# One core's decoder step: memory values projected onto rows, dt on column quarters, one memory chunk in another group

## The chip, the cores and the metric

The kernel runs as one program on one core of a Trainium2 chip. The metric is the device time of one execution in microseconds (us). TensorE (PE) does the matrix products, VectorE (DVE) and ScalarE (ACT) the elementwise work, GpSimd (POOL) only issues transfers here, and SyncE (SP) issues the loads of the weights.

## The reference

A two-layer decoder step over 320 tokens (256 of a prompt, 64 of eight samples), all in float32. Cut to what the change touches:

```python
h = rmsnorm(x)
z, xbc, dt_raw, q, k, v, g = split(h @ w_in)
dt = softplus(dt_raw + dt_bias)              # 16 heads
xbc = silu(causal_conv(xbc, ...))            # 12 slices of 128 channels
... SSD scan (uses the running sum of dt * A), retention, new states ...
x = x + concat(y_ssd, y_ret) @ w_out
mem_k = mem @ w_mk;  mem_v = mem @ w_mv      # 256 memory rows, 1024 columns each; both are outputs
x = x + cross_attend(rmsnorm(x), mem_k, mem_v)
x = x + hier_moe(rmsnorm(x))
```

## The kernel before

Activations lie with features on the 128 partitions and the 320 tokens along the free axis. All weights come as one stream of pieces of 2 MB ("quads"), numbered `q` in the order in which SP loads them into a ring of three slots (some more slots later in the layer). SP works through the list strictly in order: before a load it waits until the slot that the quad goes to is free (`freed[s]`). PE waits for `loaded[s]` in `quad(...)`, and frees a slot with the first matmul that follows its last use (`free`, `first`). A product of `h` with 128 weight columns is 8 matmuls of 128x320 in `products` (L563).

**dt.** After the 12 products for xBC, 8 matmuls with 16 weight columns each (L618) give dt_raw, then `project(Q_Z, ...)` goes on with z. ACT copies dt_raw out of PSUM, DVE does softplus and the running sum on 16 partitions (L1653 to L1678), and then the 12 convolutions (L1687, L1691).

**The memory chunks.** mem_k and mem_v are 16 products of 8 matmuls of 128x256 each, called chunks 0 to 15 here. PE does them in `project_memory(n)`, strewn as filler between the small steps of the states; ACT copies each out (L1306). Chunks 0 to 3 use quad 12, 4 to 7 quad 14, 8 to 11 quad 17, 12 to 15 quad 19. Between these, quads 13, 15, 16 and 18 hold the samples' incoming states. In the ring of three, quad 17 takes the slot of quad 14, quad 18 that of 15, and quad 19 that of 16, so quad 17 can be loaded only when chunk 7 is done.

**The four groups of sample states** (k = 0 to 3, the loop ahead of L881). In each, PE runs `from_states(k)` (L825), `new_states(k, 0)` (L857 or L860), a memory chunk, `turn_off(k)` (8 transposes, L837), `new_states(k, 1)`, with one more chunk behind k = 0 and one inside k = 3. `new_states` with running number u waits for `s_newst`, DVE's `state_half` of number u - 1 (L1874, or L1880 and L1887), since it writes the same PSUM banks. When DVE is through with a state quad, it frees its slot.

**mem_v.** Chunks 8 to 15 give mem_v with features on partitions; attention needs it with memory rows on partitions. So `turn_values` turns it with 4 times 4 transposes on PE (L902) between the products of `w_out` (L917), and ACT copies the turned parts to `v_mem`.

Of the kernel before, what the change touches and what calls it, by code (L numbers as in the profile page):

```python
# [19 lines left out]
ACT = mybir.ActivationFunctionType  # L20
# [3 lines left out]
P = 128  # L24
# [134 lines left out]
def build(nc, stream, params, consts, x_in, mem_in, y_out, st_out, conv_out, mk_out, mv_out):  # L159
    with ExitStack() as ctx:  # L160
# [3 lines left out]
        def sem(name):  # L164
            return ctx.enter_context(nc.semaphore(name))
# [70 lines left out]
        wide = view(work, 5376, 3, GB * P)  # L236
        vt_mem = view(work, 16196, KD, M)

        v_mem = view(work, 0, 2, D)
        q_all = view(work, 2048, KD, T)  # L240
# [120 lines left out]
        s_mkvout = sem("s_mkvout")  # L361
        s_vt = sem("s_vt")
        s_vtout = sem("s_vtout")
        s_mkstore = sem("s_mkstore")
# [161 lines left out]
        def _(pe):  # L526
# [56 lines left out]
            def mixer(L):  # L583
# [309 lines left out]
                project_memory(16 - n_mem)  # L893
                pe.wait_ge(s_mkvout, (L + 1) * 16)

                def turn_values(i):

                    mc, half = i // 2, i % 2
                    if i >= 2:
                        pe.wait_ge(s_vtout, L * 4 + i - 1)  # L900
                    for c in range(4):
                        mm = pe.transpose(psum[:, 4 + half, c * P:(c + 1) * P],  # L902
                                          vt_mem[:, 4 * half + c, mc * P:(mc + 1) * P], ident)
                        if c == 0:
                            first(mm)
                    mm.then_inc(s_vt, 1)

                for j in range(KD):
                    w = quad(pe, L, Q_OUT + j // 2)
                    if j >= 4:  # L910
                        pe.wait_ge(s_xadd, L * 16 + j - 3)
                    for i in range(2 * KD):
                        if j == 0 and i % KD == 0:
                            pe.wait_ge(s_mix, L * 2 + i // KD + 1)
                        a = (j % 2) * 2 * SLAB + i * P
                        src = xbc[:, i, :] if i < KD else kq[:, i - KD, :]
                        mm = pe.matmul(psum[:, j % 4, 0:T], w[:, a:a + P], src, start=(i == 0), stop=(i == 15))  # L917
                        if i == 0:
                            first(mm)
                    mm.then_inc(s_wout, 1)  # L920
                    if j % 2 == 1:
                        free(Q_OUT + j // 2)
                    if 2 <= j < 6:
                        turn_values(j - 2)

            def attention(L):

                pe.wait_ge(s_vtout, (L + 1) * 4)

# [339 lines left out]
        def _(act):  # L1269
# [22 lines left out]
            def mixer(L):  # L1292
# [7 lines left out]
                def memory(chunks):  # L1300
                    nonlocal n_mem
                    for _ in range(chunks):
                        c = n_mem
                        act.wait_ge(s_mkv, L * 16 + c + 1)
                        dst = k_mem[:, c, :] if c < KD else vt_mem[:, c - KD, :]
                        act.activation(dst, memory_out(c), ACT.Copy).then_inc(s_mkvout, 1)  # L1306
                        n_mem += 1
                nt = 0
# [14 lines left out]
                for c in range(CC):  # L1323
# [6 lines left out]
                    n_evac += 1  # L1330
                evac(dt_tmp[0:H, 0, :], rows_=H)

# [129 lines left out]
                for j in range(KD):  # L1462
                    if 2 <= j < 6:
                        i = j - 2
                        act.wait_ge(s_vt, L * 4 + i + 1)
                        act.activation(v_mem[:, i // 2, (i % 2) * BANK:(i % 2 + 1) * BANK], psum[:, 4 + i % 2, :],
                                       ACT.Copy).then_inc(s_vtout, 1)
                    act.wait_ge(s_xadd, L * 16 + j + 1)
                    square(L, 1, j)
# [105 lines left out]
        def _(dve):  # L1575
# [31 lines left out]
            def mixer(L):  # L1607
# [72 lines left out]

                for c in range(CC):
                    dve.wait_ge(s_evac, L * 29 + c + 1)
                    if c >= 2:
                        dve.wait_ge(s_silu, L * CC + c - 1)
                    a = conv_acc[:, c % 2, :]
                    wa, ba = PAT["conv_w"] + c * CW, PAT["conv_b"] + c
                    dve.tensor_scalar(a, raw[:, c, 0:XOUT], par[:, L, wa:wa + 1], par[:, L, ba:ba + 1],  # L1687
                                      ALU.mult, ALU.add)
                    for j in range(1, CW):
                        dve.drain()  # L1690
                        ins = dve.scalar_tensor_tensor(out=a, in0=raw[:, c, j:j + XOUT],  # L1691
                                                       scalar=par[:, L, wa + j:wa + j + 1], in1=a,
                                                       op0=ALU.mult, op1=ALU.add)
                    ins.then_inc(s_conv, 1)
                dve.tensor_copy(conv_tail[:, :, 0:CW - 1], raw[:, :, XS0 - (CW - 1):XS0])
# [470 lines left out]
        def _(pool):  # L2166
            for L in range(DEPTH):
# [24 lines left out]
                pool.wait_ge(s_mkvout, L * 16 + 8)  # L2192
                pool.dma_start(mk_out[L], k_mem[:]).then_inc(s_mkstore, 16)
                pool.wait_ge(s_mkvout, L * 16 + 16)
                pool.dma_start(mv_out[L], vt_mem[:]).then_inc(s_mvstore, 16)
            for i in range(3):
# [115 lines left out]
```

## Time and profile before

| | |
|---|---|
| median of 3 runs | 1607.63 us (1606.44 to 1610.14) |
| the profiled execution, whole | 1604.76 us |
| its span, first to last instruction | 1603.0 us |
| PE busy | 1535.9 us, 96% of the span |
| DVE, ACT busy | 539.6 us, 292.4 us |
| mean granted TensorE clock | 0.989 |
| loaded and stored in all | 387.77 MB, mean 242 GB/s |

The profiled execution lies 2.87 us under the median of the runs. Busy time of PE counts an instruction from its start to its modelled end. The two layers are alike; layer 0 has its state groups at 280 to 323 us, layer 1 at 1069 to 1112 us. In counts of PE rows, a matmul and its weight load are two instructions: x16 is 8 matmuls.

### The profile page before, as it was taken

The page shows a single profiled execution, that of the slowest core. Times are in us where ns is not written, and L with a number is a line of the kernel's source. Part 1 is how long each engine was busy: PE and PEld are TensorE (multiplying, and loading weights), DVE is VectorE, ACT ScalarE, POOL GpSimd, SP SyncE. Part 2 cuts the span into 40 slices and gives each one's busy share as a digit, 9 for nine tenths or more (in the row PEclk, how much of TensorE's full clock was granted, in tenths as well). Part 3 has the DMA queues.
Part 4 walks back from the last instruction along what each step waited for, and adds up shares of the span by engine and source line. Part 5 has one row for each costly group of instructions (what it writes and reads, how often), then busy time and mean ns, then how long its engine had stood idle before and what let it go on. Part 6 is the DMA issues. An engine that isn't in the chain of part 4 may idle for free.

```text
span 1603.0 us, 20261 instructions
## 1 busy us (share of the span) xinstructions
PE 1535.9 (96%) x8652; PEld 979.8 (61%) x8652; DVE 539.6 (34%) x1110; ACT 292.4 (18%) x614; POOL 28.0 (2%) x56
## 2 busy tenths in 40 slices
PE   7999999899999999999999998998999999999997
PEld 5776668577766554445367776685776675444543
DVE  3304654561132411211323065636412423121122
ACT  2013322140121301001100142212311212000102
POOL 0000000000000000000000000000000000000000
PEclk9999999999999999999999999998999999999999
DMA  7233322884267599999723242329733757999991
GB/s 312 105 117 146 136 93 101 320 326 173 105 244 302 234 414 404 404 402 410 283 80 131 105 159 97 132 106 358 298 139 135 303 212 315 403 404 409 408 395 60
DMA packets 31262, 387.77 MB, mean 242 GB/s; under 512 B 3776, under 2 KB 4224, under 8 KB 6592
## 3 DMA queue, kind: packets, MB, share of 16 engines
q1 hardware_dynamic: 26048, 357.74, 56.8%
q0 software_dynamic: 5120, 28.69, 4.5%
q8 instruction: 70, 1.15, 0.3%
q14 instruction: 24, 0.20, 0.0%
HBM read 361.66 MB, written 24.75 MB: 241 GB/s over the span
## 4 chain that ended last, share of the span: by engine, by line
PE 92%; DVE 3%; DMA 2%; ACT 1%; DVEq 1%; issue 1%; ACTq 0%; SPq 0%
PE psum L563 38%; PE psum L1139 14%; PE psum L917 9%; PE psum L1159 7%; PE psum L1184 5%; PE psum L1114 4%; DMA ring<-stream 2%; PE psum L579 1%; PE psum L570 1%; PE psum L1125 1%; PE psum L951 1%; PE psum L996 1%; PE psum L1014 1%; PE psum L967 1%; PE psum L764 1%; PE psum L576 1%
## 5 line engine op out<-in xcount | busy, mean ns | idle before, releaser
L563 PE MATMUL psum<-h,ring 128*128 128x320 f32 x1664 | 458.9, 436 | 0.9 <-issue 0.9
L563 PEld LDWEIGHTS psum<-h,ring 128*128 128x128 f32 x1664 | 315.8, 191 | 135.7 <-issue 9.2
L1139 PE MATMUL psum<-ring,work 128*64 128x512 f32 x768 | 170.3, 592 | 1.4 <-ACT work L1529 1.4
L563 PE MATMUL psum<-mem,ring 128*128 128x256 f32 x512 | 120.6, 391 | 7.2 <-DMA ring<-stream 7.2
L1139 PEld LDWEIGHTS psum<-ring,work 128*64 128x64 f32 x768 | 55.0, 137 | 110.2 <-issue 108.5
L563 PEld LDWEIGHTS psum<-mem,ring 128*128 128x128 f32 x512 | 97.8, 195 | 28.2 <-DMA ring<-stream 8.3
L1159 PE MATMUL psum<-work 128*64 128x512 f32 x512 | 113.4, 595 | 0.7 <-ACT work L1540 0.7
L917 PE MATMUL psum<-work,ring 128*128 128x320 f32 x384 | 104.9, 433 | 0.9 <-ACT work L1306 0.9
L917 PEld LDWEIGHTS psum<-work,ring 128*128 128x128 f32 x384 | 72.3, 190 | 30.9 <-ACT work L1306 1.8
L563 PE MATMUL psum<-work,ring 128*128 128x320 f32 x256 | 71.9, 443 | 11.7 <-DMA ring<-stream 10.5
L2062 DVE TENSOR_TENSOR x<-x,psum 128x320 f32<-128x320 f32 x128 | 62.5, 488 | 54.9 <-PE psum L1184 49.2
L1159 PEld LDWEIGHTS psum<-work 128*64 128x64 f32 x512 | 35.3, 137 | 67.5 <-issue 66.3
L1594 DVE TENSOR_TENSOR x<-x,psum 128x320 f32<-128x320 f32 x32 | 15.6, 488 | 175.7 <-PE psum L917 123.6
L1184 PE MATMUL psum<-work 128*128 128x320 f32 x256 | 73.2, 439 | 0.5 <-issue 0.5
L563 PEld LDWEIGHTS psum<-work,ring 128*128 128x128 f32 x256 | 49.8, 195 | 33.0 <-issue 13.7
L2107 DVE TENSOR_TENSOR work<-work,psum 128x512 f32<-128x512 f32 x16 | 11.0, 688 | 173.4 <-ACT work L1538 173.4
L1114 PEld LDWEIGHTS psum<-work 128*128 128x128 f32 x512 | 60.0, 196 | 13.7 <-issue 13.7
L1184 PEld LDWEIGHTS psum<-work 128*128 128x128 f32 x256 | 47.2, 190 | 31.5 <-issue 13.6
L1114 PE MATMUL psum<-work 128*128 128x128 f32 x512 | 63.0, 283 | 2.2 <-DVE work L2053 2.2
L1538 ACT ACTIVATE work<-psum 128x512 f32<-128x512 f32 x16 | 9.6, 597 | 285.6 <-PE psum L1139 285.6
L1139 PE MATMUL psum<-states_out,work 128*64 128x512 f32 x256 | 58.4, 598 | 0.0
L1326 ACT ACTIVATE work<-psum 128x256 f32<-128x256 f32 x24 | 9.2, 385 | 216.8 <-PE psum L563 216.8
(296 smaller groups left out, 1387.6 us busy)
## 6 DMA issues: line engine op xcount, KB each, us to landing
ring<-stream SPq DMA_DIRECT2D x111, 2048.0 KB, 11.0
work<-stream SPq DMA_DIRECT2D x32, 2048.0 KB, 9.9
states_out<-stream SPq DMA_DIRECT2D x24, 2048.0 KB, 9.6
st_out<-states_out POOLq DMA_DIRECT2D x12, 1024.0 KB, 11.4
st_out<-work POOLq DMA_DIRECT2D x6, 1024.0 KB, 7.5
work<-acum_flat POOLq DMA_DIRECT2D x10, 256.0 KB, 3.9
k_mem<-acum_flat POOLq DMA_DIRECT2D x10, 256.0 KB, 3.5
ring<-stream SPq DMA_DIRECT2D x4, 512.0 KB, 9.2
```

The source lines that it names most:

```text
L563: mm = pe.matmul(out, w[:, a:a + P], rhs[:, j, :], start=(j == 0), stop=(j == KD - 1))
L570: mm = pe.transpose(o, i, ident[0:i.shape[0], 0:i.shape[0]])
L576: return pe.transpose(out, src[:, cols(t)], ident)
L579: mm = pe.matmul(out[32 * j:32 * j + DS, :], src[:, own:own + DS], ident, start=True, stop=True, skip_group_check=True)
L764: mm = pe.matmul(o, x_of[t][:, hd * HD:(hd + 1) * HD], dec[:, 0, hh * n:(hh + 1) * n], start=True, stop=(t != 1), skip_group_check=True)
L917: mm = pe.matmul(psum[:, j % 4, 0:T], w[:, a:a + P], src, start=(i == 0), stop=(i == 15))
L951: mm = pe.matmul(psum[:, t, rr * M:(rr + 1) * M], q_all[:, k, tok(t)], k_mem[:, k, :], start=(c == 0), stop=(c == 1))
L1114: mm = pe.matmul(psum[:, 4 + half, i * P:(i + 1) * P], h_tok[:, t, j * P:(j + 1) * P], chosen[:, p, t, :], start=(i + t == 0), stop=False, ...
L1139: mm = pe.matmul(psum[ab * CAP:(ab + 1) * CAP, up, :], h_packed[:, p % 2, k, ab * CAP:(ab + 1) * CAP], w[:, a:a + BANK], start=(k == 0), s ...
L1159: mm = pe.matmul(psum[ab * CAP:(ab + 1) * CAP, 2 + half, :], hidden_t[:, f, ab * CAP:(ab + 1) * CAP], w[:, a:a + BANK], start=(f == 0), st ...
L1184: pe.matmul(psum[:, SPREAD[j % 4], 0:T], y_pair[:, j * P:(j + 1) * P], picked_t, start=True, stop=True).then_inc(s_spread, 1)
L2062: dve.tensor_tensor(x[:, j, :], x[:, j, :], psum[:, SPREAD[j % 4], 0:T], ALU.add)\
```

## The change

It has three parts, the same in both layers.

1. **Values on rows.** The weights of mem_v are laid out in another order, and chunks 8 to 15 become eight half sums of 4 matmuls of 128x512: 128 memory rows are the stationary side, 512 columns of `w_mv` stream. Two chunks together give one block of `v_mem` in its final layout, and ACT copies only after each second chunk. `v_mem` takes the place in SBUF that the unturned values had. The 16 transposes of `turn_values`, their waits and their copies are gone. The same number of columns streams as before.
2. **dt on quarters.** The 8 matmuls of dt write four quarters of the PSUM partitions, two sums in each. ACT copies all 128 rows, PE does the first z product meanwhile, then adds up the quarters in one more matmul with a constant (`fold`), and ACT copies its 16 rows. DVE does convolutions 0 and 1 ahead of the dt chain instead of behind it.
3. **One chunk moves.** The extra chunk behind group k = 0 now stands behind group k = 2. The chunks keep their order, so group 0 has chunk 5, group 1 chunk 6, and group 2 chunks 7 and 8 (before: 5 and 6, 7, and 8).

```diff
 def memory_out(c):
     if c < 2:
         return psum[:, 0, 0:M]
-    return psum[:, 7, 0:M] if c >= 6 and c % 2 == 0 else psum[:, 4, M:2 * M]
+    if c >= KD:
+        return psum[:, (7, 4)[(c - KD) // 2 % 2], :]
+    return psum[:, 7, 0:M] if c == 6 else psum[:, 4, M:2 * M]
...
 # TensorE, dt
-    mm = pe.matmul(psum[0:H, n_proj % 4, 0:T], w[:, j * H:(j + 1) * H], h[:, j, :],
-                   start=(j == 0), stop=(j == KD - 1))
+    q = 32 * (j % 4)
+    mm = pe.matmul(psum[q:q + H, n_proj % 4, 0:T], w[:, j * H:(j + 1) * H], h[:, j, :],
+                   start=(j < 4), stop=(j >= 4), skip_group_check=True)
...
-project(Q_Z, range(2))
+project(Q_Z, [0])
+pe.wait_ge(s_tables, 16)
+pe.wait_ge(s_evac, L * 29 + 13)
+pe.matmul(psum[0:H, 4, 0:T], k_("fold", H), dt_tmp[:, 5, :], start=True, stop=True).then_inc(s_dtfold, 1)
+project(Q_Z, [1])
+pe.wait_ge(s_dtrow, L + 1)
...
 # TensorE, project_memory
-elif c > 6:
-    pe.wait_ge(s_mkvout, L * 16 + c - 1)
-products(memory_out(c), w, (c % 4) * SLAB, P, mem).then_inc(s_mkv, 1)
+elif 6 < c < KD:
+    pe.wait_ge(s_mkvout, L * 12 + c - 1)
+elif c >= KD and c % 2 == 0:
+    pe.wait_ge(s_mkvout, L * 12 + 7 + (c - KD) // 2)
+if c < KD:
+    products(memory_out(c), w, (c % 4) * SLAB, P, mem).then_inc(s_mkv, 1)
+else:
+    mt = (c - KD) // 2 % 2
+    for k in range(4 * (c % 2), 4 * (c % 2) + 4):
+        mm = pe.matmul(memory_out(c), mem[:, k, mt * P:(mt + 1) * P],
+                       w[:, k * BANK:(k + 1) * BANK], start=(k == 0), stop=(k == KD - 1),
+                       skip_group_check=True)
+        if k % 4 == 0:
+            first(mm)
+    if c % 2 == 1:
+        mm.then_inc(s_mkv, 1)
...
 # TensorE, the groups of states
     new_states(k, 1)
-    if k == 0:
+    if k == 2:
         project_memory(1)
...
 # TensorE, between the products of w_out
-        if 2 <= j < 6:
-            turn_values(j - 2)
...
 # ScalarE
-evac(dt_tmp[0:H, 0, :], rows_=H)
+evac(dt_tmp[:, 5, :])
+act.wait_ge(s_dtfold, L + 1)
+act.activation(dt_tmp[0:H, 0, :], psum[0:H, 4, 0:T], ACT.Copy).then_inc(s_dtrow, 1)
...
-memory(3)
+memory(2)
 act.activation(gate[:], gate[:], ACT.Silu)
 off_to_tok(2)
-memory(2)
+memory(3)
...
 # VectorE
+convolve(0)
+convolve(1)
 dve.wait_ge(s_proj, L * 45 + 29)
...
-dve.wait_ge(s_evac, L * 29 + 13)
+dve.wait_ge(s_dtrow, L + 1)
```

PE's rows in the groups of states, from `new_states(0, 1)` to `new_states(2, 1)`, before. Here `mem,ring 128x256 x8` is a chunk, L825 is `from_states`, L837 is `turn_off`, and L857 and L860 are `new_states`.

```order
L857 MATMUL psum<-states_out 128x256 x8
L563 MATMUL psum<-mem,ring 128x256 x8
L825 MATMUL psum<-ring,work 8x512 x8
L860 MATMUL psum<-h 128x512 x4
L563 MATMUL psum<-mem,ring 128x256 x8
L837 MATMUL psum<-cst,h 128x128 x8
L860 MATMUL psum<-h 128x512 x4
L825 MATMUL psum<-ring,h 8x256 x16
L857 MATMUL psum<-work 128x256 x8
L563 MATMUL psum<-mem,ring 128x256 x8
L837 MATMUL psum<-cst,h 128x128 x8
L857 MATMUL psum<-work 128x256 x8
```

The same stretch in the changed kernel, where L568 and L714 are chunks, L850 is `from_states`, L862 `turn_off`, and L882 and L885 `new_states`.

```order
L882 MATMUL psum<-states_out 128x256 x8
L850 MATMUL psum<-ring,work 8x512 x8
L885 MATMUL psum<-h 128x512 x4
L568 MATMUL psum<-mem,ring 128x256 x8
L862 MATMUL psum<-cst,h 128x128 x8
L885 MATMUL psum<-h 128x512 x4
L850 MATMUL psum<-ring,h 8x256 x16
L882 MATMUL psum<-work 128x256 x8
L568 MATMUL psum<-mem,ring 128x256 x8
L862 MATMUL psum<-cst,h 128x128 x8
L882 MATMUL psum<-work 128x256 x8
L714 MATMUL psum<-ring,mem 128x512 x4
```

Between `new_states(0, 1)` and `from_states(1)` the chunk is gone; chunk 7, the last user of quad 14, now stands behind `new_states(2, 0)`, and chunk 8, the first of quad 17, behind `new_states(2, 1)`.

PE's rows around dt before, from xBC's products to the first transposes of the values of retention (L576, L579); L618 is dt.

```order
L563 MATMUL psum<-h,ring 128x320 x160
L618 MATMUL psum<-h,ring 16x320 x8
L563 MATMUL psum<-h,ring 128x320 x16
L576 MATMUL psum<-cst,work 128x128 x16
L579 MATMUL psum<-cst,work 8x128 x64
```

And in the changed kernel, where L624 is dt and L634 the matmul with `fold`.

```order
L568 MATMUL psum<-h,ring 128x320 x160
L624 MATMUL psum<-h,ring 16x320 x8
L568 MATMUL psum<-h,ring 128x320 x8
L634 MATMUL psum<-work,cst 16x320
L568 MATMUL psum<-h,ring 128x320 x8
L581 MATMUL psum<-cst,work 128x128 x16
```

One z product now stands between dt and the matmul that completes it, and one behind.

## Rows read from the trace of the kernel before

**Rows 1.** The page: busy time by engine, and the chain that ended last.

```profile
PE 1535.9 (96%) x8652; PEld 979.8 (61%) x8652; DVE 539.6 (34%) x1110; ACT 292.4 (18%) x614; POOL 28.0 (2%) x56
...
PE 92%; DVE 3%; DMA 2%; ACT 1%; DVEq 1%; issue 1%; ACTq 0%; SPq 0%
```

**Rows 2.** Stages: busy time by engine; last three: granted clock, DMA share, GB/s.

```profile
283.00:323.00 40.00, 32.42 (x238) 21.14 (x231) 24.66 (x22) 6.70 (x8) 3.21 (x6) 0.91 0.80 306
308.00:310.00 2.00, 0.00 (x0) 0.00 (x0) 1.43 (x2) 0.00 (x0) 0.24 (x1) 0.64 0.97 406
546.00:800.00 254.00, 250.04 (x1337) 120.18 (x1338) 59.02 (x121) 28.56 (x49) 0.00 (x0) 1.00 0.94 381
```

**Rows 3.** The chain that ended last, in time: start, length, what; both layers.

```profile
299.44 11.73 DMA ring<-stream
...
1089.77 11.23 DMA ring<-stream
```

**Rows 4.** PE's timeline, groups of states, layer 0; in brackets the wait ahead.

```profile
302.19 1.91 PE L825 MATMUL psum<-ring,h 128*8 128x256 f32 x32 [0.45 <-DMA ring<-stream]
305.77 1.15 PE L857 MATMUL psum<-work 8*128 8x256 f32 x16 [1.67 <-DVEq L1888]
311.22 5.76 PE L563 MATMUL psum<-mem,ring 128*128 128x256 f32 x16 [4.30 <-DMA ring<-stream]
...
321.50 1.14 PE L860 MATMUL psum<-work 8*128 8x512 f32 x8 [0.74 <-DVEq L1888]
```

**Rows 5.** The chain, in time: widths 512 and 256, and products of w_out.

```profile
246.26 1.73 PE psum L704 x4
...
343.94 10.37 PE psum L563 x48
...
381.31 8.61 PE psum L917 x32
390.37 8.62 PE psum L917 x32
```

**Rows 6.** PE's timeline, the same stretch, layer 1.

```profile
1096.09 2.09 PE L857 MATMUL psum<-work 8*128 8x256 f32 x16 [0.67 <-DVEq L1888]
1101.04 5.10 PE L563 MATMUL psum<-mem,ring 128*128 128x256 f32 x16 [2.86 <-DMA ring<-stream]
...
1110.66 1.14 PE L860 MATMUL psum<-work 8*128 8x512 f32 x8 [0.30 <-DVEq L1888]
```

**Rows 7.** Timelines: dt on PE, routing's column quarters on PE, DVE at dt.

```profile
134.04 4.48 PE L618 MATMUL psum<-h,ring 128*16 128x320 f32 x16
...
533.97 1.27 PE L1073 MATMUL psum<-work,par 128*20 128x320 f32 x14
...
139.01 0.37 DVE L1653 TENSOR_SCALAR work<-work,par 16x320 f32<-16x320 f32 x1 [29.28 <-ACT work L1313]
```

**Rows 8.** DVE's timeline, groups of states, layer 0.

```profile
289.23 2.35 DVE L1874 SCALAR_TENSOR_TENSOR states_out<-ring,psum 128x1024 f32<-128x1024 f32 x2 [0.69 <-PE psum L857]
291.80 2.29 DVE L1925 TENSOR_TENSOR work<-work 128x2048 f32<-128x2048 f32 x1 [0.21 <-issue]
...
303.40 2.29 DVE L1887 TENSOR_TENSOR work<-work,psum 128x2048 f32<-128x2048 f32 x1
```

**Rows 9.** Transfers issued 243-244, 299-301, 305-308, 347.3-348: KB, us to landing.

```profile
ring<-stream SPq DMA_DIRECT2D x1, 2048.0 KB, 7.7
...
ring<-stream SPq DMA_DIRECT2D x1, 2048.0 KB, 11.7
...
ring<-stream SPq DMA_DIRECT2D x1, 2048.0 KB, 12.7
...
states_out<-stream SPq DMA_DIRECT2D x1, 2048.0 KB, 8.2
ring<-stream SPq DMA_DIRECT2D x1, 2048.0 KB, 13.9
```

More of the change, by code:

```diff
@@ L236, in build @@
         wide = view(work, 5376, 3, GB * P)
-        vt_mem = view(work, 16196, KD, M)
-        v_mem = view(work, 0, 2, D)
+        v_mem = view(work, 16196, 2, D)
         q_all = view(work, 2048, KD, T)
@@ L312, in build @@
         s_rotated = sem("s_rotated")
+        s_dtfold = sem("s_dtfold")
+        s_dtrow = sem("s_dtrow")
         s_dtv = sem("s_dtv")
@@ L361, in build @@
         s_mkvout = sem("s_mkvout")
-        s_vt = sem("s_vt")
-        s_vtout = sem("s_vtout")
         s_mkstore = sem("s_mkstore")
@@ L463, in memory_out, with memory_taken @@
                 return psum[:, 0, 0:M]
-            return psum[:, 7, 0:M] if c >= 6 and c % 2 == 0 else psum[:, 4, M:2 * M]
+            if c >= KD:
+                return psum[:, (7, 4)[(c - KD) // 2 % 2], :]
+            return psum[:, 7, 0:M] if c == 6 else psum[:, 4, M:2 * M]
+        def memory_taken(c):
+            return c if c <= KD else KD + (c - KD) // 2
         def place_of(step):
@@ L893, in mixer @@
                 project_memory(16 - n_mem)
[L894 to L906, printed above, removed]
+                pe.wait_ge(s_mkvout, (L + 1) * 12)
                 for j in range(KD):
@@ L1303, in memory @@
                         c = n_mem
-                        act.wait_ge(s_mkv, L * 16 + c + 1)
-                        dst = k_mem[:, c, :] if c < KD else vt_mem[:, c - KD, :]
+                        n_mem += 1
+                        if c >= KD and c % 2 == 0:
+                            continue
+                        act.wait_ge(s_mkv, L * 12 + memory_taken(c + 1))
+                        u = (c - KD) // 2
+                        dst = k_mem[:, c, :] if c < KD else v_mem[:, u % 2, (u // 2) * BANK:(u // 2 + 1) * BANK]
                         act.activation(dst, memory_out(c), ACT.Copy).then_inc(s_mkvout, 1)
-                        n_mem += 1
                 nt = 0
@@ L1462, in mixer @@
                 for j in range(KD):
[L1463 to L1467, printed above, removed]
                     act.wait_ge(s_xadd, L * 16 + j + 1)
@@ L1647, in mixer, with convolve @@
                                     w[:, a:a + DB * (CW - 1)].rearrange("p (b j) -> p b j", b=DB))
+                def convolve(c):
+                    dve.wait_ge(s_evac, L * 29 + c + 1)
+                    if c >= 2:
+                        dve.wait_ge(s_silu, L * CC + c - 1)
+                    a = conv_acc[:, c % 2, :]
+                    wa, ba = PAT["conv_w"] + c * CW, PAT["conv_b"] + c
+                    dve.tensor_scalar(a, raw[:, c, 0:XOUT], par[:, L, wa:wa + 1], par[:, L, ba:ba + 1],
+                                      ALU.mult, ALU.add)
+                    for j in range(1, CW):
+                        dve.drain()
+                        ins = dve.scalar_tensor_tensor(out=a, in0=raw[:, c, j:j + XOUT],
+                                                       scalar=par[:, L, wa + j:wa + j + 1], in1=a,
+                                                       op0=ALU.mult, op1=ALU.add)
+                    ins.then_inc(s_conv, 1)
+                dve.drain()
+                convolve(0)
+                convolve(1)
                 dve.wait_ge(s_proj, L * 45 + 29)
@@ L1679, in mixer @@
                     .then_inc(s_dtv, 1)
[L1681 to L1694, printed above, removed]
+                for c in range(2, CC):
+                    convolve(c)
                 dve.tensor_copy(conv_tail[:, :, 0:CW - 1], raw[:, :, XS0 - (CW - 1):XS0])
@@ L2191, in _ @@
                     pool.dma_start(st_out[L, 1 + u], new_of[STORE_SLOT[u]]).then_inc(s_store[STORE_SLOT[u]], 16)
-                pool.wait_ge(s_mkvout, L * 16 + 8)
+                pool.wait_ge(s_mkvout, L * 12 + 8)
                 pool.dma_start(mk_out[L], k_mem[:]).then_inc(s_mkstore, 16)
-                pool.wait_ge(s_mkvout, L * 16 + 16)
-                pool.dma_start(mv_out[L], vt_mem[:]).then_inc(s_mvstore, 16)
+                pool.wait_ge(s_mkvout, (L + 1) * 12)
+                pool.dma_start(mv_out[L], v_mem[:]).then_inc(s_mvstore, 16)
             for i in range(3):
@@ L2245 @@
                  state_ret[l].transpose(2, 0, 1, 3).reshape(P, GB, 4, 1024)]
-        st[Q_MEM] = quads(slabs(np.concatenate([f(w_mk)[l], f(w_mv)[l]], 1)))
+        st[Q_MEM[:2]] = quads(slabs(f(w_mk)[l]))
+        st[Q_MEM[2:]] = f(w_mv)[l].reshape(KD, P, 2, BANK).transpose(2, 1, 0, 3).reshape(2, P, QUAD)
         for k, (ret, gb) in enumerate(STATES):
@@ L2286 @@
     outs = {"y_out": (P, KD, T), "st_out": (DEPTH, 1 + DB, P, 2048), "conv_out": (DEPTH, P, CC, (CW - 1) * (1 + DB)),
-            "mk_out": (DEPTH, P, KD, M), "mv_out": (DEPTH, P, KD, M)}
+            "mk_out": (DEPTH, P, KD, M), "mv_out": (DEPTH, P, 2, D)}
     nc = bacc.Bacc("TRN2", target_bir_lowering=False, num_devices=1)
@@ L2310 @@
     return (c(y[:SEQ].reshape(1, SEQ, D)), c(y[SEQ:].reshape(DB, DS, D)), c(ssm[:, :1]), c(conv[:, :1]), c(ret[:, :1]),
-            c(memory(r["mk_out"])), c(memory(r["mv_out"])), c(ssm[:, 1:]), c(conv[:, 1:]), c(ret[:, 1:]))
+            c(memory(r["mk_out"])),
+            c(np.asarray(r["mv_out"]).transpose(0, 2, 1, 3).reshape(DEPTH, 1, M, XH, DV)), c(ssm[:, 1:]), c(conv[:, 1:]), c(ret[:, 1:]))
```

3 lines of the change are left out of this document (1 added, 2 removed).

## Prediction

> **What bounds the kernel now.** I read the page first. PE is busy for 96% of the span, and 92% of the chain that ended last lies on it [rows 1]: whatever PE is spared in a busy stage comes off the time, and whatever it waits longer is added. In the experts' stage it is busy for 250 of 254 us [rows 2], so nothing done earlier is given back or made up there; it just begins earlier or later.
>
> The table by stage then shows the one place that is different. In the groups of states, 283 to 323 us, PE is busy for 32.4 of 40 us and transfers move 306 GB/s [rows 2]. The chain there runs through a load of the ring: 11.73 us from 299.44 in layer 0, and 11.23 us from 1089.77 in layer 1 [rows 3]. That load is quad 17, issued when chunk 7 was done. PE's timeline shows what it costs: `new_states(2, 0)` begins at 305.77, held by DVE, and then PE stands still for 4.30 us until chunk 8 can begin at 311.22 [rows 4]. Chunk 8 takes 5.76 us, where three chunks in a row take 10.37, so 3.46 each [rows 4, 5]: the granted clock, 0.64 in the mean of 308 to 310 [rows 2], has fallen to the lower level, 1.2 GHz, after PE had stood idle, and rises again during the chunk. The reader should see that the whole change hangs on this load, since the moved chunk is tied to it.
>
> As the mark by which I compare I take the end of `new_states(3, 0)`: 321.50 + 1.14 = 322.6 in layer 0 and 1110.66 + 1.14 = 1111.8 in layer 1 [rows 4, 6]. Before and after the change the same chunks remain behind it.
>
> **dt on quarters.** The 8 matmuls of 16 columns take 4.48 us [rows 7], as much as full ones. In the routing of the experts 7 matmuls of 20 columns already go to four quarters, and take 1.27 us [rows 7]; 8 would take 1.45. The added `fold` matmul has the same 320 columns as one of the old ones: 4.48 / 8 = 0.56. PE saves 4.48 - 1.45 - 0.56 = 2.5 us a layer, 5.0 in all. The new waits cost nothing while a z product hides them: it is 8 matmuls of 320 columns, so about 4.4 us, and ACT's copy of dt behind it is one instruction; without that cover it would be a copy's time twice a layer. DVE gets dt about 1.45 + 4.4 + 0.56 - 4.48 = 1.9 us later on the layer's clock. It had been idle for 29.28 us before dt [rows 7], and convolutions 0 and 1 now fall into that gap, so what follows dt starts no later.
>
> The Trainium skill ("TensorEngine Tiling (Array Packing)", Key Properties) says that a change of tiling mode drains the engine, which speaks against quarters between full products. Routing's 7 matmuls stand between full products too, and their 1.27 us leave room for 0.29 of overhead at most if they stream at a quarter of 0.56 each. By the page without a price I could not sum; by the row the saving stays.
>
> **Values on rows.** 32 matmuls of 512 columns replace 64 of 256. Two of 512 took 1.73 us [rows 5], so four take 3.46: exactly a chunk of eight. No gain, no loss on PE. What is gone is the turning: between two products of `w_out` there is a gap of 390.37 - 381.31 - 8.61 = 0.45 us [rows 5], four times a layer, so 1.75 us a layer and 3.5 in all. ACT loses its copies, which nothing waited for in time; its last copy ahead of `w_out` gets twice as wide, some tenths of a us that I count at nothing. Bounds of these two parts together: 7.0 (if `fold` and its waits cost twice) to 9.5; I take 8.5.
>
> **The moved chunk.** Group 0 has one chunk less, group 2 one more. Three things follow in order.
>
> First, nothing moves earlier for DVE. From 289.23 its state work runs almost without a break until 303.40 + 2.29 = 305.7 [rows 8], so `new_states(2, 0)` still begins at 305.8, and PE, a chunk short in groups 0 and 1, waits more for it. Second, chunk 7 now runs behind it: 305.77 + 1.15 + 3.46 = 310.4. Only then is the slot of quad 14 free, so quad 17 is issued at 310.4 instead of 299.44, eleven us later. SP takes its list in order, so quad 18, the states of group 3, is held behind it and is issued at 310.4 as well. Third, PE does `turn_off(2)` and `new_states(2, 1)` and stands at chunk 8 from about 312.4.
>
> How long do the two loads take? Alone a load landed after 7.7 us; quads 17 and 18 took 11.7 and 12.7 with stores of new states beside them; of two issued together the first landed after 8.2 and the second after 13.9, 5.7 apart [rows 9]. Here too two stores of new states go out beside them, behind `new_states(2, 0)` and `new_states(2, 1)`. I take 10.0 for quad 17, between alone and 11.7, nearer to the latter, and 15.0 for quad 18, the pair's 13.9 with a little for the stores. So quad 17 is there at 320.4, PE has been idle for 8 us, and chunk 8 at the low clock takes 5.5 (5.76 and 5.10 before [rows 4, 6]): 325.9. Quad 18 is there at 325.4. Then `from_states(3)` at 1.9 (as in [rows 4]) and `new_states(3, 0)` at 1.14, for which DVE is long ready: 328.9, or 6.3 us later than before.
>
> In layer 1 `new_states(2, 0)` begins at 1096.09. It took 2.09 there and the chunk 5.10 at the low clock [rows 6], against 1.15 and 3.46 at the high one; chunk 7 ends between 1100.7 and 1103.3, I take 1102.0. Plus 10.0, 5.1, 1.9 and 1.14: 1120.1, or 8.3 later. Together +14.6.
>
> The Trainium skill ("DMA: Bandwidth & Descriptors", Anatomy of one DMA) fits a transfer's time as 2.0 us plus its bytes at 436 GB/s. That is 6.8 us for 2 MB and 11.6 for two, both shorter than the rows' 7.7 and 13.9, and the moved chunk would then cost some 6 us less than I say. The measured rows are for this kernel's own loads, so I stay with them.
>
> Behind the mark I find no slack that takes this back: the next loads are issued by the same steps and only shift.
>
> **Sum.** +14.6 - 5.0 - 3.5 = +6.1 us on the profiled execution's 1604.76, so 1610.9. That execution lies 2.87 under the median of 1607.63; on the median's scale the sum is 1613.7 us. A measurement of this kernel can tell about 0.2%, 3.2 us, from no change.
>
> **The rivals.** What decides is the time P from the issue of quad 17 to the landing of quad 18, and the clock. At the high clock the marks come at 310.4 + P + 3.04 and 1100.7 + P + 3.04, so both layers lose 2P - 17.2 together.
>
> *The loads are quick and the clock holds.* With 7.7 and 5.7 behind it, P is 13.4; the loss of 9.6 and the gain of 8.5 cancel: 1608.7. For it speaks that the transfer queues stand nearly idle before 310 in the changed order; against it that two stores go out then, and that PE's clock fell in both layers after much less idleness. It holds up to P = 14.5.
>
> *The chunk fills the stall.* This one is faster. Chunk 7 covers the 4.30 us, and quad 17 is there when PE wants it, at 312.4. The mark would be 312.4 + 3.46 + 3.04 = 318.9, 3.7 earlier, and in layer 1 1109.2, 2.6 earlier: -6.3 - 8.5 = -14.8, so 1592.8. For it speaks that the wait is exactly where the chunk goes. Against it: the load would have to land 2 us after its slot is free. Any gain over 0.2% needs P under 11.3, and no pair in the rows was that quick.
>
> *All goes badly.* Low clock already in chunk 7 of both layers, loads of 12.7 and 5.7 behind: 334.4 and 1124.7, a loss of 24.7, net +16.2, so 1623.8.
>
> *The change doesn't do what it says for dt.* If quarters did not overlap, dt would save nothing and cost `fold`: 6.1 us worse than the sum, 1619.8. Routing's row speaks against it.
>
> **How the numbers follow.** Late loads as I sum them, with all between +3.2 and +14: 0.56. Worse than that, or dt without gain: 0.06. The loads quick, within 0.2%: 0.25. Faster, by the filled stall or by a P that I have no row for: 0.13. So slower 0.62, same 0.25, faster 0.13. The predicted time is that of the likeliest, 1613.7. The range goes from 1603 (a little into the faster cases) to 1621; the likeliest case alone has 1611 to 1621.
>
> **What the profile after would show.** Right: one wait of PE for a load at chunk 8 of about 8 us in place of 4.30 and 2.86; quad 17 issued right behind chunk 7 and quad 18 within half a us of it; the clock low at chunk 8; dt at 1.5 us with `fold` at 0.6 behind the first z product; products of `w_out` with no gaps; stage 283 to 323 longer by 6 to 8 us in both layers. Wrong: quad 17 issued before `new_states(2, 0)`, or landing within 8 us with quad 18 close behind; PE not idle at chunk 8; or a new wait at `fold` or ahead of the first transposes.

## The result, and the profile after

The changed kernel takes 1615.63 us in the median (1613.93 to 1616.82), against 1607.63 before: a ratio of 1.0051 (95% interval 1.0038 to 1.0063), 8.0 us slower. One further run took 1833.18 us at a mean granted clock of 0.839, where these four had 0.983 to 0.984, and is left out. On a second occasion (the last experiment) it took 1618.48, a ratio of 1.0068 (1.0051 to 1.0085). The profiled execution took 1615.62 us with a span of 1613.8, where before had 1603.0.

The page, busy time by engine and the chain that ended last: PE's part of the chain falls from 92% [rows 1] to 90%, and transfers gain a point.

```profile
PE 1533.9 (95%) x8496; PEld 952.2 (59%) x8496; DVE 539.8 (33%) x1110; ACT 287.8 (18%) x600; POOL 27.9 (2%) x56
...
PE 90%; DMA 3%; DVE 3%; ACT 1%; DVEq 1%; issue 1%; SPq 0%; ACTq 0%
```

PE's timeline after (start, length, what; in brackets the wait ahead). First dt and `fold`; then layer 0 from the first product of `new_states` (L882) to the mark; then the same in layer 1. L850 is `from_states`, L568 chunk 7, L714 chunk 8, L885 `new_states` of an odd group.

```profile
133.47 1.27 PE L624 MATMUL psum<-h,ring 128*16 128x320 f32 x16
...
139.18 0.71 PE L634 MATMUL psum<-work,cst 128*16 128x320 f32 x2
...
144.23 1.91 PE L581 MATMUL psum<-cst,work 128*128 128x128 f32 x16
...
279.15 1.50 PE L882 MATMUL psum<-states_out 8*128 8x256 f32 x16
...
299.73 3.60 PE L850 MATMUL psum<-ring,h 128*8 128x256 f32 x32 [0.60 <-DMA ring<-stream]
...
304.59 3.72 PE L568 MATMUL psum<-mem,ring 128*128 128x256 f32 x16
...
318.15 6.74 PE L714 MATMUL psum<-ring,mem 128*128 128x512 f32 x8 [7.90 <-DMA ring<-stream]
325.13 1.90 PE L850 MATMUL psum<-ring,work 128*8 128x512 f32 x16 [0.23 <-DMA ring<-stream]
326.96 1.14 PE L885 MATMUL psum<-work 8*128 8x512 f32 x8
...
1075.60 1.15 PE L882 MATMUL psum<-states_out 8*128 8x256 f32 x16
...
1099.56 5.18 PE L568 MATMUL psum<-mem,ring 128*128 128x256 f32 x16
...
1112.67 5.44 PE L714 MATMUL psum<-ring,mem 128*128 128x512 f32 x8 [5.98 <-DMA ring<-stream]
1119.76 1.90 PE L850 MATMUL psum<-ring,work 128*8 128x512 f32 x16 [1.66 <-DMA ring<-stream]
1121.60 1.14 PE L885 MATMUL psum<-work 8*128 8x512 f32 x8
```

The waits of 4.30 and 2.86 us at chunk 8 [rows 4, 6] have become 7.90 and 5.98. What PE waits for was issued by SP right behind chunk 7: quad 17 at 308.45 and 1104.88, and quad 18 0.37 us behind it (SP's timeline, both layers). The second row also holds quad 19, 4.45 us behind quad 17; in layer 0 it comes at 312.90, after the window shown:

```profile
308.45 1.56 SPq L507 DMA_DIRECT2D ring<-stream  x2
...
1104.88 4.78 SPq L507 DMA_DIRECT2D ring<-stream  x3
```

The chain that ended last runs through the load that is late, and this is now quad 18, not 17: it ends at `from_states(3)`, in layer 0 (first row) and in layer 1 (third row). The second row is `w_out`, 256 rows in one piece, where before it had gaps [rows 5]; the last is the experts' last down product, to which I come back.

```profile
308.82 16.27 DMA ring<-stream
...
360.32 69.17 PE psum L929 x256
...
1105.25 14.47 DMA ring<-stream
...
1586.69 8.78 PE psum L1167 x32
```

In the table by stage PE stands for all of 314 to 318 us, transfers move 385 GB/s meanwhile, and the granted clock is 0.51, the lower of its two levels; before chunk 8's wait it was 1.00.

```profile
308.00:310.00 2.00, 2.00 (x26) 1.59 (x24) 0.49 (x2) 0.38 (x1) 0.04 (x1) 1.00 0.78 319
314.00:318.00 4.00, 0.00 (x0) 0.00 (x0) 0.00 (x0) 0.00 (x0) 0.00 (x0) 0.51 1.01 385
```

To compare stretches by themselves I need where they begin and end before; PE's timeline of the kernel before (L857 is the first `new_states`, L576 the first transposes behind dt, and L917 the start of `w_out`):

```profile
147.16 1.04 PE L576 MATMUL psum<-cst,work 128*128 128x128 f32 x8
...
282.35 1.15 PE L857 MATMUL psum<-states_out 8*128 8x256 f32 x16
...
354.77 1.61 PE L917 MATMUL psum<-work,ring 128*128 128x320 f32 x5 [0.47 <-ACT work L1306]
...
1072.27 1.55 PE L857 MATMUL psum<-states_out 8*128 8x256 f32 x16
```

From the first `new_states` to the mark, "the groups" from here on, before takes 322.64 - 282.35 = 40.29 us in layer 0 and 1111.80 - 1072.27 = 39.53 in layer 1. The changed kernel takes 326.96 + 1.14 - 279.15 = 48.95 and 47.14. That is +8.66 and +7.61, 16.3 in all. From dt's start to the transposes it takes 144.23 - 133.47 = 10.76 instead of 147.16 - 134.04 = 13.12 [rows 7], so 2.4 less a layer, 4.7 in all. The four gaps between the products of `w_out`, 0.45 each [rows 5], are gone, 1.8 a layer and 3.5 in all. 16.3 - 4.7 - 3.5 = +8.1.

### The profile page after: what moved, and what is told of

Its sections match the earlier page's. It is cut to its first block, busy times and chain, and to the rows that moved or that the text cites. A ratio compares the mean times of both kernels' runs of the same rounds, so it can differ in the third digit from the quotient of the medians.

```text
span 1613.8 us, 19931 instructions
## 1 busy us (share of the span) xinstructions
PE 1533.9 (95%) x8496; PEld 952.2 (59%) x8496; DVE 539.8 (33%) x1110; ACT 287.8 (18%) x600; POOL 27.9 (2%) x56
## 4 chain that ended last, share of the span: by engine, by line
PE 90%; DMA 3%; DVE 3%; ACT 1%; DVEq 1%; issue 1%; SPq 0%; ACTq 0%
PE psum L568 34%; PE psum L1147 14%; PE psum L929 9%; PE psum L1167 7%; PE psum L1192 4%; PE psum L1122 4%; DMA ring<-stream 3%; PE psum L714 3%; PE psum L584 1%; PE psum L575 1%; PE psum L1133 1%; PE psum L959 1%; PE psum L1004 1%; PE psum L1022 1%; PE psum L975 1%; PE psum L850 1%
## 5 line engine op out<-in xcount | busy, mean ns | idle before, releaser
L568 PE MATMUL psum<-h,ring 128*128 128x320 f32 x1664 | 456.1, 434 | 0.9 <-issue 0.9
L568 PEld LDWEIGHTS psum<-h,ring 128*128 128x128 f32 x1664 | 314.3, 190 | 134.5 <-issue 7.5
L1167 PE MATMUL psum<-work 128*64 128x512 f32 x512 | 116.8, 610 | 0.7 <-ACT work L1548 0.7
L568 PE MATMUL psum<-work,ring 128*128 128x320 f32 x256 | 71.2, 440 | 11.9 <-DMA ring<-stream 10.7
L714 PE MATMUL psum<-ring,mem 128*128 128x512 f32 x128 | 62.3, 638 | 13.9 <-DMA ring<-stream 13.9
L568 PEld LDWEIGHTS psum<-work,ring 128*128 128x128 f32 x256 | 49.4, 194 | 32.8 <-issue 13.3
L568 PE MATMUL psum<-mem,ring 128*128 128x256 f32 x256 | 60.8, 392 | 0.0
L568 PEld LDWEIGHTS psum<-mem,ring 128*128 128x128 f32 x256 | 48.5, 194 | 9.9 <-issue 3.5
```

What stands on the lines that cost most here:

```text
L568: mm = pe.matmul(out, w[:, a:a + P], rhs[:, j, :], start=(j == 0), stop=(j == KD - 1))
L714: mm = pe.matmul(memory_out(c), mem[:, k, mt * P:(mt + 1) * P], w[:, k * BANK:(k + 1) * BANK], start=(k == 0), stop=(k == KD - 1), skip_gr ...
L1167: mm = pe.matmul(psum[ab * CAP:(ab + 1) * CAP, 2 + half, :], hidden_t[:, f, ab * CAP:(ab + 1) * CAP], w[:, a:a + BANK], start=(f == 0), st ...
```

## The experiments

**Which part does what.** Four kernels, timed on one chip against 18 runs of the kernel before (1607.22). First the changed kernel with its chunk back at group 0:

```diff
-    if k == 2:
+    if k == 0:
         project_memory(1)
...
-memory(2)
+memory(3)
 act.activation(gate[:], gate[:], ACT.Silu)
...
-memory(3)
+memory(2)
```

> Values on rows and dt on quarters as in the changed kernel, the chunk back behind group 0. Theory (the moved chunk alone lengthens the groups of states, by 8.3 and 8.0 us, since quads 17 and 18 come late): 1607.6 - 4.7 - 3.5 = 1599.4 us, within 3; chunk 8 waits some 4 us for its load again. Rival (the wide half sums of the values or dt lengthen the groups too, the move only part of it): the groups stay some 4 us longer in each layer, 1607 us or more.

Measured: 1602.18 us (1599.07 to 1602.46), ratio 0.9958 (0.9944 to 0.9972). It beats both kernels. Its PE timeline, layer 0: the wait at chunk 8 is 2.96, and the mark comes 38.93 us behind `new_states(0, 0)`, which began at 281.63.

```profile
309.63 5.27 PE L714 MATMUL psum<-ring,mem 128*128 128x512 f32 x8 [2.96 <-DMA ring<-stream]
...
319.42 1.14 PE L885 MATMUL psum<-work 8*128 8x512 f32 x8 [0.21 <-DVEq L1902]
```

Then the move alone, the same lines the other way round on the kernel before:

```diff
-    if k == 0:
+    if k == 2:
         project_memory(1)
```

> The kernel before with only the chunk moved from group 0 to group 2. Theory: both layers' groups 8 us longer, 1607.6 + 16 = 1623.9 us, between 1620 and 1627; PE waits about 8 us at chunk 8. Rival (the loss needs the wide half sums): 1611 to 1615 us.

Measured: 1622.83, ratio 1.0092 (1.0077 to 1.0108), so +14.8 us (12.4 to 17.4). The groups take 48.10 and 48.64, +16.9 in all. Its chain runs through the same late load, in layer 0:

```profile
311.72 16.21 DMA ring<-stream
```

Then dt on quarters alone (with `fold` and the order of the convolutions), and values on rows alone, each on the kernel before:

```diff
-    mm = pe.matmul(psum[0:H, n_proj % 4, 0:T], w[:, j * H:(j + 1) * H], h[:, j, :],
+    q = 32 * (j % 4)
+    mm = pe.matmul(psum[q:q + H, n_proj % 4, 0:T], w[:, j * H:(j + 1) * H], h[:, j, :],
...
-project(Q_Z, range(2))
+project(Q_Z, [0])
+pe.wait_ge(s_evac, L * 29 + 13)
+pe.matmul(psum[0:H, 4, 0:T], k_("fold", H), dt_tmp[:, 5, :], start=True, stop=True).then_inc(s_dtfold, 1)
+project(Q_Z, [1])
```

> The kernel before with only dt on quarters, its fold, and two convolutions ahead. Theory: 2.4 us less in each layer, 1607.6 - 4.7 = 1602.9 us, within 2.5. Rival (the earlier start shifts where the clock falls, or the fold's waits hold other work): 1606 to 1610 us.

```diff
-products(memory_out(c), w, (c % 4) * SLAB, P, mem).then_inc(s_mkv, 1)
+if c < KD:
+    products(memory_out(c), w, (c % 4) * SLAB, P, mem).then_inc(s_mkv, 1)
+else:
+    mt = (c - KD) // 2 % 2
+    for k in range(4 * (c % 2), 4 * (c % 2) + 4):
+        mm = pe.matmul(memory_out(c), mem[:, k, mt * P:(mt + 1) * P], w[:, k * BANK:(k + 1) * BANK],
...
-        if 2 <= j < 6:
-            turn_values(j - 2)
```

> The kernel before with only the values projected onto rows, the chunk unmoved. Theory: the four turnings of 0.45 us are gone in each layer, 1607.6 - 3.5 = 1604.1 us, within 2.5, and chunk 8 waits some 4 us as before. Rival (a half sum of four wide matmuls at the low clock takes longer than a chunk of eight): the groups 2 us longer in each layer, 1608 us.

Measured: 1603.27, ratio 0.9977 (0.9967 to 0.9988), and 1603.62, ratio 0.9978 (0.9967 to 0.9988): -3.7 and -3.5 us. The parts add up: 0.9977 x 0.9978 = 0.9955, where both together gave 0.9958, and 0.9958 x 1.0092 = 1.0050, where the whole change gave 1.0051.

**What of the moved chunk costs it.** The theory is the chain of the prediction: chunk 7 frees the slot of quad 14 late, and quads 17 and 18 are then loaded while PE stands. Three kernels, on one chip against 29 runs of before (1607.14). In the first quads 17 and 18 change slots, so that quad 17 goes where quad 15 was and needs not wait for chunk 7; quad 18 does instead:

```diff
 def slot_of(q):
...
+    if q in (17, 18):
+        return (0, 2)[q - 17]
```

> The changed kernel, but quad 17 (chunk 8) goes to the slot of quad 15 and quad 18 (states of group 3) to that of quad 14: quad 17 no longer waits for chunk 7. Theory (the groups are longer since the load of quad 17 is tied to chunk 7): quad 17 is issued some 6 us sooner, PE's wait at chunk 8 shrinks from 7.9 to about 2 us, and quad 18, no longer behind it, lands 3 to 4 us sooner in each layer: 1615.6 - 7 = 1608.6 us, within 3. Rival (the loss is in the order of PE's small steps, with no filler in group 1): no change, 1615.6 us within 2.

Measured: 1613.03 (1606.36 to 1619.19), ratio 1.0042 (1.0028 to 1.0056), more than the 1608.6 within 3 that was expected. Layer 0 came as expected, 45.04 us for the groups, 3.9 less than in the changed kernel; layer 1 gained nothing clear, 1119.08 - 1071.19 = 47.9, where the two profiles of the changed kernel have 47.1 and 49.0. PE's timeline, both layers (L716 is chunk 8, L852 `from_states`, L570 chunk 7):

```profile
314.93 5.40 PE L716 MATMUL psum<-ring,mem 128*128 128x512 f32 x8 [2.42 <-DMA ring<-stream]
...
1095.91 6.34 PE L570 MATMUL psum<-mem,ring 128*128 128x256 f32 x16
...
1104.17 3.70 PE L716 MATMUL psum<-ring,mem 128*128 128x512 f32 x8
1113.45 3.60 PE L852 MATMUL psum<-ring,work 128*8 128x512 f32 x16 [5.58 <-DMA ring<-stream]
```

In layer 1 chunk 8 no longer waits at all, but chunk 7 ran at the low clock and freed quad 18's slot late, so the wait went to `from_states(3)`. One of the two loads goes to the slot that chunk 7 frees, in either deal of these two slots.

The second loads only half of both quads (chunk 8 and group 3 then compute on what the other halves of the slots held before):

```diff
-sp.dma_start(slots[s], stream[L * QUADS + q]).then_inc(loaded[s], 16)
+n_col = QUAD // 2 if q in (17, 18) else QUAD
+sp.dma_start(slots[s][:, 0:n_col], stream[L * QUADS + q][:, 0:n_col]).then_inc(loaded[s], 16)
```

> The changed kernel with only the first half of quads 17 and 18 loaded (the rest of these weights and states is left out). Theory (the landing of these loads ends the wait): quad 17 lands some 2.5 us sooner and quad 18 some 5 us; the mark comes 3 to 4 us sooner in each layer, held by chunk 8 at the low clock: 1608.6 us, within 3. Rival (stores or the order of small steps hold PE, not these loads): no change, 1615.6 us.

Measured: 1611.42, ratio 1.0020 (1.0004 to 1.0036), so 4 to 5 us less than the changed kernel on its first occasion and 7 less than on its second, at the upper edge of what was expected. The groups take 44.47 and 44.69. The wait at chunk 8 (L715) is 4.73, and `from_states(3)` behind it waits for nothing:

```profile
317.23 6.53 PE L715 MATMUL psum<-ring,mem 128*128 128x512 f32 x8 [4.73 <-DMA ring<-stream]
```

The third puts the chunk behind group 1, so that chunk 7 ends one group earlier:

```diff
-    if k == 2:
+    if k == 1:
         project_memory(1)
```

> The changed kernel with the moved chunk behind group 1, halfway. Theory (the later chunk 7 ends, the later quads 17 and 18): quad 17 is issued some 5 us later than with the chunk behind group 0, the groups are 4 to 5 us longer than there: 1602 + 9 = 1611 us, within 3. Rival (what counts is whether chunk 7 stands ahead of the second wait for DVE): as with the chunk behind group 0, 1602 us.

Measured: 1609.59 (1601.82 to 1616.31), ratio 1.0011 (0.9995 to 1.0026), as expected; the groups 44.84 and 45.35. How late chunk 7 stands sets the cost: 40.0 us for the groups with the chunk at group 0 (mean of both layers of the kernel without the move and of the kernels with dt or values alone), 45.1 behind group 1, 48.3 behind group 2 (both profiles). Chunk 8 still waits:

```profile
312.02 5.64 PE L714 MATMUL psum<-ring,mem 128*128 128x512 f32 x8 [5.25 <-DMA ring<-stream]
```

**Is it the idle time or the low clock behind it?** Matmuls whose results nothing uses fill the wait at chunk 8, first 16:

```diff
+if c == KD:
+    pe.wait_ge(s_mkvout, L * 12 + 8)
+    for i in range(16):
+        pe.matmul(psum[:, 4, 0:M], mem[:, i % KD, 0:P], mem[:, (i + 1) % KD, :], start=True, stop=True)
```

> The changed kernel with 16 more matmuls of 128x256 (results unused) ahead of the wait for quad 17, so that PE is busy for 6.9 of the 7.9 us. Theory (quad 18, landing about when chunk 8 ends, binds as much as the low clock does): chunk 8 takes 3.6 in place of 6.7 and 5.4 us, PE then waits for quad 18 instead, and the marks move by under 0.5 us: 1615.6 us, within 2. Rival (the low clock after idleness costs what it shows): 2 to 3 us less a layer, 1610.5 us.

Measured: 1621.96 (1620.45 to 1624.81), ratio 1.0088 (1.0074 to 1.0103): a miss of 6 us. In layer 0 the filling ended 2.17 us before quad 17 was there, so chunk 8 was slow all the same (L702 is the filling, L719 chunk 8, L855 `from_states(3)`), and the groups took 49.26:

```profile
311.70 7.17 PE L702 MATMUL psum<-mem 128*128 128x256 f32 x32
321.04 5.40 PE L719 MATMUL psum<-ring,mem 128*128 128x512 f32 x8 [2.17 <-DMA ring<-stream]
327.70 1.90 PE L855 MATMUL psum<-ring,work 128*8 128x512 f32 x16 [1.26 <-DMA ring<-stream]
```

In layer 1 they took 51.24, with `from_states(2)` and chunk 7, ahead of the filling, already at the low clock. A second execution of the same kernel with a profile, and a kernel with 22 matmuls (`range(22)`) that close the gap:

> The same kernel as with 16 additional matmuls, one look more. In the first profile layer 1 was longer than in the changed kernel (51.2 us for the groups), with the clock already low ahead of the additional matmuls. If that fall is chance, layer 1 is now 47 to 49 us with the clock high until chunk 7, and the time is nearer to 1616; if it belongs to the kernel, the same rows come again: from_states(2) at 3.6 and chunk 7 at over 6 us in layer 1, and 1620 to 1625.

> The changed kernel with 22 additional matmuls of 128x256 (their results are not used), 9.5 us at the high clock, ahead of chunk 8's wait for quad 17, six more than in the earlier filled kernel, so that TensorE is busy until about when quad 17 lands. Theory (quad 18's landing binds the stage, and the low clock only hides in that wait): chunk 8 takes about 3.6 us, then TensorE waits 2.5 to 3 us for quad 18 ahead of from_states(3); from the start of new_states(0, 0) to the end of new_states(3, 0) layer 0 takes 48 to 49.5 us as in the changed kernel, and the time stays at 1615.6, within 3 us; up to 1622 if the additional work costs something by itself, as the kernel with 16 may say. Rival (the low clock in chunk 8 costs its 2 to 3 us a layer): the groups at 46 us in both layers, the time near 1610.

The second execution took 1624.03 us, and neither guess fits it quite: the groups took 53.71 in layer 0 this time and 50.29 in layer 1, with the low clock in layer 0 at `from_states(2)`, chunk 7 (5.32) and, now that chunk 8 was fast, `from_states(3)`:

```profile
298.57 3.60 PE L855 MATMUL psum<-ring,h 128*8 128x256 f32 x32 [2.34 <-DMA ring<-stream]
...
325.66 3.60 PE L855 MATMUL psum<-ring,work 128*8 128x512 f32 x16 [3.36 <-DMA ring<-stream]
```

With 22 it took 1621.38 (1615.16 to 1625.56), ratio 1.0080 (1.0059 to 1.0102), whose interval overlaps both of the changed kernel's. The groups 49.15 and 48.31, as the theory said:

```profile
321.56 3.60 PE L719 MATMUL psum<-ring,mem 128*128 128x512 f32 x8
327.95 1.90 PE L855 MATMUL psum<-ring,work 128*8 128x512 f32 x16 [2.80 <-DMA ring<-stream]
```

Chunk 8 at the high clock is 6.74 - 3.60 = 3.1 us shorter, and 2.80 of this goes into a wait for quad 18. So the low clock in chunk 8 costs nothing in this stretch; the landing of quad 18 sets its end. What the added matmuls cost in the whole time, 3 to 8 us, stays open. The profile with 22 has most of it in front of the groups, where the kernels are alike: 136.7 and 137.4 us from the first transposes behind dt to the groups, where the changed kernel has 134.9 and 135.1 in its first profile, 136.9 and 135.3 in its second.

**Can the wait at chunk 8 be had for less?** The kernel with the chunk at group 0, with quad 17 in two loads that signal apart:

```diff
+elif q == Q_MEM[2]:
+    sp.dma_start(slots[s][:, 0:2 * SLAB], stream[L * QUADS + q][:, 0:2 * SLAB]).then_inc(s_vhalf, 16)
+    sp.dma_start(slots[s][:, 2 * SLAB:], stream[L * QUADS + q][:, 2 * SLAB:]).then_inc(loaded[s], 16)
...
+if c == KD:
+    pe.wait_ge(s_vhalf, 16 * (L + 1))
+    w = slots[slot_of(Q_MEM[2])]
```

> The kernel with dt on quarters and values on rows and the chunk where it was before, with quad 17 loaded by two transfers of half the size that signal apart, so that chunk 8, which reads only the first half, begins on that. Theory: chunk 8 begins 2 to 3 us earlier and its wait is gone or under 1 us, but quad 18 then binds about 1 us later, so 1 to 1.5 us a layer are saved: 1599 to 1600 against 1602.2 without the split. Rival (the whole wait and the low clock behind it are saved, since quad 18 has room): 3 us a layer, 1596. Other rival (two transfers of half the size share the queues, and the first half lands no sooner than the whole): 1602.

Measured: 1604.43 (1596.90 to 1608.46), ratio 0.9977 (0.9964 to 0.9991): no gain over 1602.18. The groups take 41.30 and 42.67, longer than 38.93 and 39.91 without the split. Chunk 8 (L722) does begin at once, but PE then waits in one piece for quad 18 at `from_states(3)` (L858), which comes out at the low clock:

```profile
302.66 3.70 PE L722 MATMUL psum<-ring,mem 128*128 128x512 f32 x8
...
314.73 3.60 PE L858 MATMUL psum<-ring,work 128*8 128x512 f32 x16 [6.41 <-DMA ring<-stream]
```

**Does the loss repeat?** The changed kernel as it is, once more:

> The changed kernel itself once more, on another occasion, with a second profile, since the two profiles of the filled kernel differed by 4 us in one stretch. Theory (the waits for quads 17 and 18 make the loss in every execution, and the clock's falls elsewhere come by chance): from the start of new_states(0, 0) to the end of new_states(3, 0) 47 to 49.5 us in both layers, chunk 8 behind a wait of 6 to 8 us, and a time of 1613 to 1617 us. Rival (the first profile was a chance draw, and the moved chunk alone usually costs less): groups at 45 to 46 us in both layers and 1609 to 1611 us.

Measured: 1618.48 (1617.79 to 1620.63), ratio 1.0068 (1.0051 to 1.0085), so the loss repeats, 1.5 us above the upper end of the expected time; the groups 48.14 and 48.96, as expected. PE's timeline, the same rows as of the first profile:

```profile
282.15 1.15 PE L882 MATMUL psum<-states_out 8*128 8x256 f32 x16
...
320.34 6.71 PE L714 MATMUL psum<-ring,mem 128*128 128x512 f32 x8 [7.84 <-DMA ring<-stream]
327.32 1.90 PE L850 MATMUL psum<-ring,work 128*8 128x512 f32 x16 [0.27 <-DMA ring<-stream]
...
1077.99 1.15 PE L882 MATMUL psum<-states_out 8*128 8x256 f32 x16
...
1102.71 6.36 PE L568 MATMUL psum<-mem,ring 128*128 128x256 f32 x16
...
1116.96 6.06 PE L714 MATMUL psum<-ring,mem 128*128 128x512 f32 x8 [5.94 <-DMA ring<-stream]
1123.98 1.90 PE L850 MATMUL psum<-ring,work 128*8 128x512 f32 x16 [0.96 <-DMA ring<-stream]
```

SP issued its two loads at 310.69 and 1109.21:

```profile
310.69 1.56 SPq L507 DMA_DIRECT2D ring<-stream  x2
...
1109.21 0.80 SPq L507 DMA_DIRECT2D ring<-stream  x2
```

## Why the prediction was right, step by step

**The moved chunk** was right in mechanism and order, and nearly in size. The three things that were to follow did: `new_states(2, 0)` no earlier, quads 17 and 18 issued together behind chunk 7, PE standing at chunk 8 for 7.90 us (forecast: about 8). The stretch splits into three pieces, each worked out from the rows above: from the first `new_states` to the issue of quad 17, from there to `from_states(3)`, and from there to the mark. "Forecast" is the prediction's own working, set from the start of the groups before.

| us | to the issue | to `from_states(3)` | to the mark | the groups |
|---|---|---|---|---|
| layer 0, forecast | 310.4 - 282.35 = 28.05 | 15.5 | 3.04 | 46.6 |
| first profile | 29.30 | 16.68 | 2.97 | 48.95 |
| second profile | 28.54 | 16.63 | 2.97 | 48.14 |
| layer 1, forecast | 1102.0 - 1072.27 = 29.73 | 15.1 | 3.04 | 47.9 |
| first profile | 29.28 | 14.88 | 2.98 | 47.14 |
| second profile | 31.22 | 14.77 | 2.97 | 48.96 |

The term that was too small is P in layer 0, 16.7 us where I took 15.0. Two things had been left out of it. The pair's 13.9 [rows 9] counts from the second issue, 0.37 us behind the first (347.41 and 347.04), so on P's own scale that pair took 14.3; the row of the first, in SP's timeline before:

```profile
347.04 0.33 SPq L502 DMA_DIRECT2D states_out<-stream  x1
```

And quad 19, issued 4.45 us behind quad 17, was under way beside the pair, as well as the stores. What it costs no run shows; layer 1 has it too, with a P of 14.9.

The sum also took another path than the kernel. It let the end of chunk 8 (325.9 and 1117.1) set `from_states(3)`, with quad 18 there 0.5 and 0.1 us earlier. In both profiles and both layers `from_states(3)` waits for quad 18 instead, by 0.23, 1.66, 0.27 and 0.96 us behind chunk 8. The two ends lie so close together that the size hardly changes.

Also `from_states(2)` came out at the low clock in the first profile, 3.60 where it had 1.91 [rows 4], which covers the 1.25 by which the first column is over. In layer 0 the forecast was +6.3 and the first profile says +8.7, in layer 1 +8.3 and +7.6; the second says +7.9 and +9.4. Timed by itself the move costs 14.8 us (12.4 to 17.4), against 14.6 forecast. The stretches say 16.3 and 17.3 in all, and 16.9 with the move alone, so that so close an agreement is partly luck.

Quad 17 landed after 318.15 - 308.45 = 9.70 us in layer 0 and 7.79 in layer 1, where I took 10.0. By the fit in the Trainium skill ("DMA: Bandwidth & Descriptors", Anatomy of one DMA), which the page gives for transfers that GpSimd issues, 2 MB would take an estimated 6.8 us and both together 11.6. With the stores of states and quad 19 beside them the traces show 9.7 and 16.7 in layer 0 and 7.8 and 14.9 in layer 1, so that fit is too quick for these loads of SP's by 1 to 5 us.

**dt** gave 2.4 us a layer in the profile, forecast 2.5: the eight matmuls took 1.27 (forecast 1.45), `fold` 0.71 (0.56), and no wait stands ahead of `fold` or of the transposes. The page on "TensorEngine Tiling (Array Packing)" in the Trainium skill (Key Properties) speaks of a drain at a change of mode. If the eight stream at a quarter of 0.56 each, the row's 1.27 us leave room for 0.15 of it at most. Timed alone the part gave 3.7 (1.9 to 5.3) of the 5.0. **Values on rows** closed its four gaps, 1.8 a layer as forecast, and by itself gave 3.5, as forecast.

**What lies behind the mark** moved with it unchanged: from the mark to `w_out` before has 354.77 - 322.64 = 32.13 us, after 360.32 - 328.10 = 32.22, and the experts' stage is as busy as before (251.2 of 254 us from 550 on).

**The rivals.** *The chunk fills the stall* needed P under 11.3; P was 14.8 to 16.7. It is refuted, and so is its reason: the wait stands where the chunk went, but the chunk is what the load waits for. *The loads are quick and the clock holds* needed P up to 14.5; layer 1 comes within 0.4 us of that, layer 0 does not, and chunk 8 was slow in both (6.74 and 5.44). That part of it, though, would have mattered little: the kernel with 22 matmuls shows chunk 8 at the high clock and the same end. *All goes badly* asked for the low clock already in chunk 7 of both layers; it was there in layer 1 (5.18 and 6.36), not in layer 0. *dt does nothing* is refuted by its rows.

**The sum** was +6.1; the stretches say +8.1, the medians +8.0, and the second occasion +10.8. The 10.8 us between the two spans hold 2.7 more than the stretches. The clock also fell at other places in the profiled execution, such as the experts' last down product, 8.75 and 8.78 us in the two layers where before has 7.09. The second profile of the same kernel has 8.74 and 7.09, and the kernel with the chunk back at group 0 has 7.09 and 8.78, so this does not come with the moved chunk.

## What to carry to other kernels

Work that fills a wait has to be looked at as a user of buffers as well: if it is the last user of the slot that the awaited load goes to, moving it into the wait makes the wait longer, and everything that the queue holds behind that load moves with it. Look for which of two loads lands last before taking away the first wait: here a fast chunk 8 and an early quad 17 only passed the wait on to quad 18, and other slots did so in one of the two layers. And time the parts of a change apart: two of the three gained some 3.5 us each, and without the third the kernel is faster than before, 1602.18 us.

## What the runs showed of the hardware

The granted clock falls at other places from one execution of the same kernel to the next. The experts' last down product, in the chain of the changed kernel's second profile, against 8.78 in its first:

```profile
1591.94 7.09 PE psum L1167 x32
```

The groups of the kernel with 16 added matmuls took 49.26 and 53.71 us in layer 0 in two profiles. Some kernels also spread more than others: 1606 to 1619 with other slots, where 29 runs of the kernel before beside it lay between 1604 and 1610; why is not shown. So 2 to 4 us of one profile may be chance, and a stretch has to be compared over several profiles.

The same pair of loads took 16.7 and 16.6 us in layer 0, and 14.9 and 14.8 in layer 1, in both profiles. In layer 0 POOL issued a store of states just ahead of the pair; in layer 1, where chunk 7 ran slowly, 2.4 us earlier (POOL's timeline, first profile):

```profile
307.51 0.53 POOL L2205 DMA_DIRECT2D st_out<-states_out  x1 [4.53 <-DVEq L1902]
...
1102.45 0.53 POOL L2205 DMA_DIRECT2D st_out<-states_out  x1 [3.38 <-DVEq L1902]
```

It does not go by the layer: in the kernel with the move alone the store stood 0.9 us ahead of the pair in both layers, and quad 18 landed 16.6 and 16.7 us behind the issue of quad 17. Over six profiles (both of the changed kernel, the move alone, and the three with added matmuls) the seven pairs with a store 0.9 us ahead took 16.6 to 17.7 us, and the five with 2.3 to 3.8 us took 14.7 to 16.0. That the store is the cause is argued, not tested.
